# The second block's input projection as three fp32r products of split operands

## What is computed

```
xn = rmsnorm(h, g_mix)                      # 512 x 1024
z  = xn @ w_in + b_in                       # 1024 -> 1536
a, gate, p = z[:, :512], z[:, 512:1024], z[:, 1024:]
# conv group: GLU -> causal depthwise conv, 31 taps -> LayerNorm -> swish
u = a * sigmoid(gate); v = conv31(u) + b_dw; y_conv = silu(layernorm(v))
# pool group: 4 groups of 128 channels, trailing mean over 2, 4, 8, 16 tokens minus the token, then a 128x128 map
h = h + concat(y_conv, y_pool) @ w_out
h = h + swiglu(rmsnorm(h, g_ffn)); out = rmsnorm(h, g_final)
```

## Time and profile before

| what | value |
|---|---|
| median of 3 runs (lowest, highest) | 2475.74 us (2472.94, 2476.06) |
| the profiled execution: own time, span | 2474.01 us, 2472.2 us |
| granted PE clock, mean over the span | 0.892 of full |
| PE busy | 2221.1 us, 90% of the span |
| DVE busy | 627.3 us, 25% |
| ACT busy | 425.2 us, 17% |
| POOL busy | 32.7 us, 1% |

### The profile page before, as it was taken

How to read it: one execution, slowest core, us unless ns; L and a number is a source line. 1 busy time by engine, 2 the same in 40 slices (tenths; PEclk the granted TensorE clock), 3 DMA queues, 4 the chain that set the end, 5 groups by cost and what they waited for, 6 DMA issues and landing times.

```text
span 2472.2 us, 20613 instructions
## 1 busy us (share of the span) xinstructions
PE 2221.1 (90%) x8798; PEld 1295.5 (52%) x8798; DVE 627.3 (25%) x1011; ACT 425.2 (17%) x654; POOL 32.7 (1%) x42
## 2 busy tenths in 40 slices
PE   4977999899887898989989898989998998999997
PEld 2544454444574444444444444444343466888785
DVE  4251324232222111111111111011102943222233
ACT  2133534410010000000000000000011023222222
POOL 0000000000000000000000000000003000000000
PEclk9988999998787888888988888888989998999998
DMA  8210111034633897979979797989974113323210
GB/s 303 68 35 17 51 35 52 17 111 153 247 136 148 342 396 319 385 320 401 398 316 394 315 388 317 385 342 392 391 316 165 53 34 103 102 86 102 85 51 34
DMA packets 143792, 513.44 MB, mean 208 GB/s; under 512 B 7891, under 2 KB 70355, under 8 KB 107731
## 3 DMA queue, kind: packets, MB, share of 16 engines
q1 hardware_dynamic: 141632, 503.35, 52.8%
q10 hardware_dynamic: 2070, 8.78, 0.9%
HBM read 510.00 MB, written 2.10 MB: 207 GB/s over the span
## 4 chain that ended last, share of the span: by engine, by line
PE 88%; DVE 6%; ACT 3%; issue 2%; DMA 1%; POOL 0%; SPq 0%; ACTq 0%; DVEq 0%; POOLq 0%
PE ps L878 18%; PE ps L411 13%; PE ps L910 11%; PE ps L839 9%; PE ps L416 6%; PE ps L1053 5%; PE ps L1012 3%; PE ps L1014 3%; PE ps L1013 3%; PE ps L860 2%; PE ps L621 2%; DMA ring<-in_ada_w 1%; DVE work L1745 1%; PE ps L566 1%; PE ps L676 1%
## 5 line engine op out<-in xcount | busy, mean ns | idle before, releaser
L411 PE MATMUL ps<-work,ring 128*128 128x512 f32 x784 | 344.0, 597 | 0.8 <-DVE work L1589 0.8
L878 PE MATMUL ps<-work 128*64 128x512 f32 x1136 | 288.1, 595 | 0.0
L839 PE MATMUL ps<-work 128*128 128x64 f32 x1024 | 218.2, 416 | 62.8 <-DVE work L1712 62.8
L839 PEld LDWEIGHTS ps<-work 128*128 128x128 f32 x1024 | 215.2, 326 | 76.1 <-DVE work L1712 76.1
L411 PEld LDWEIGHTS ps<-work,ring 128*128 128x128 f32 x784 | 149.1, 192 | 187.3 <-issue 185.6
L878 PE MATMUL ps<-ring,work 128*64 128x512 f32 x912 | 238.1, 592 | 0.0
L878 PEld LDWEIGHTS ps<-work 128*64 128x64 f32 x1136 | 97.2, 138 | 158.3 <-issue 158.1
L1322 ACT ACTIVATE work<-ps 64x512 f32<-64x512 f32 x64 | 32.6, 585 | 749.1 <-PE ps L878 749.1
L878 PEld LDWEIGHTS ps<-ring,work 128*64 128x64 f32 x912 | 80.0, 137 | 126.7 <-issue 126.7
L416 PE MATMUL ps<-ring,work 128*128 128x256 f32 x640 | 142.0, 385 | 0.9 <-ACT work L1351 0.9
L1012 PE MATMUL ps<-xh,wh 128*128 128x512 f32 x352 | 138.0, 392 | 1.0 <-issue 1.0
(11 more groups left out here) (229 smaller groups left out, 2027.9 us busy)
## 6 DMA issues: line engine op xcount, KB each, us to landing
work<-in_w_exp_gate SPq DMA_DIRECT2D x71, 1024.0 KB, 12.7
work<-in_w_exp_up SPq DMA_DIRECT2D x71, 1024.0 KB, 10.8
ring<-in_w_exp_down SPq DMA_DIRECT2D x64, 1024.0 KB, 15.4
work<-in_w_exp_down SPq DMA_DIRECT2D x64, 1024.0 KB, 15.1
ring<-in_w_exp_up SPq DMA_DIRECT2D x57, 1024.0 KB, 9.6
ring<-in_w_exp_gate SPq DMA_DIRECT2D x57, 1024.0 KB, 11.7
ring<-in_w_in SPq DMA_DIRECT2D x27, 1024.0 KB, 7.6
ring<-in_ada_w SPq DMA_DIRECT2D x24, 1024.0 KB, 5.8
```

Source lines behind the costliest of these rows:

```text
L411: i = e.matmul(bank(bk), piece(key)[:, off + k, 128 * j:128 * j + 128], rhs(k), start=(k == 0), stop=(k == nk - 1))
L839: p = e.matmul(bank(5 - k // 4, 64, 64 * (k % 4)), at(XS2 + 1024 * c + 128 * k, 128), at(OH[z] + 64 * c, 64), start=(c == 0), stop=(c == 3))
L878: p = e.matmul(PS[64 * gu:64 * gu + 64, fb, :], at(XET[z] + 64 * k, 64), flat(key)[:, 512 * fb:512 * fb + 512], start=(k == 0), stop=(k == 7))
```

## The change

Each fp32 matmul of the projection becomes three fp32r matmuls: high part of the weights times high part of `xn`, high times low, and low times high (`dense_i2`, in place of `dense_T`). The parts are made so:

- `IH`, eight 128x512 blocks, on ACT, and `IL` (the rest `xn - IH`) on DVE, in the loop that copies `xn(k)` out of PSUM. `IL` takes the room of `xn` itself.
- the high part of each weight piece, `i2_hi(n)` on ACT, into one of two rooms of 128x2048 (`IWH`); the second of them is slot 5 of the ring.
- the low part, `i2_lo(n)`, in place in the piece's slot: pieces 0 and 1 on DVE, pieces 2 to 5 on GpSimd behind the 31 diagonal matrices.

A unit of PE waits for the low part of its piece, and u0 also waits block by block for `IL`. `i2_hi(n)` for n of 2 and more waits until PE is done with piece n - 2. The tail of the ring plan uses slots 0 to 4 for the first ten pieces, and SP waits for all twelve units before it loads `("ff", 0)` into slot 5. The places in ACT's program: `i2_hi(0)` ahead of the loop over k, `i2_hi(1)` behind it, 2, 3 and 4 ahead of the sigmoids of the second, third and fourth GLU pair, 5 behind the fourth.

```diff
--- before.py
+++ after.py
@@ -90,6 +90,9 @@
 YP = PSB + 2048 + 64
 PLT = [YP + 2048, YP + 2048 + 544]
 XS3, XS4 = U, XNT
+IXH = PLT[1] + 544
+IWH = [IXH + 4096, SLOT[5]]
+assert IWH[0] + W <= AR
 HIDO = WORK
 TQ = HIDO + FT * 512
 XHO = TQ + 2048
@@ -127,7 +130,7 @@
     cycle = (10, 11, 12, 5, 0, 3, 1, 2, 4, 6, 7, 8, 9)
     slots += [cycle[i % 13] for i in range(len(ex))]
     tail = [("i2", c) for c in (3, 1, 2, 0, 5, 4)] + [("o2", n) for n in range(4)] + [("ff", f) for f in range(33)]
-    slots += [i % 6 for i in range(len(tail))]
+    slots += [0, 1, 2, 3, 4, 0, 1, 2, 3, 4] + [(5, 0, 1, 2, 3, 4)[i % 6] for i in range(33)]
     keys += ex + tail
     uses, plan = {}, {}
     before = {}
@@ -180,7 +183,7 @@
     "mg_ga mg_gb mg_pa mg_pb mg_sa mg_sb mg_a mg_b mg_m ar_pe ar_a ad_d "
     "wo_pe wo_t wo_x rt_pe rt_e rt_d "
     "x_g x_oh x_xa x_xd x_ow x_ot x_oc x_gu x_sl x_hd x_ht x_hc x_dn x_ym x_cb x_ca "
-    "pads dg i2_pe gl_sg gl_u cv_pe cv_a cv_d pw_in pw_o po_pe po_y mu_pe dv sqv vr_pe ln_a y_d y_a "
+    "ix_h ix_l iw_h iw_d iw_p pads dg i2_pe gl_sg gl_u cv_pe cv_a cv_d pw_in pw_o po_pe po_y mu_pe dv sqv vr_pe ln_a y_d y_a "
     "o2_pe o2_x sx_h sx_l fs_h fs_l fs_p ff_pe ff_s ff_m hs_h hs_l dn_pe dn_e fin_x fin_a fin_o"
 ).split()
 
@@ -250,6 +253,9 @@
         XH, XL = part("xh", XHO, 4096), part("xl", XLO, 4096)
         WH = [part(f"wh{i}", WO + 4096 * i, 2048) for i in range(2)]
         WL = [part(f"wl{i}", WO + 4096 * i + 2048, 2048) for i in range(2)]
+        IH, IL = part("ih", IXH, 4096), part("il", XNT, 4096)
+        IWHI = [part(f"iwh{i}", o, 2048) for i, o in enumerate(IWH)]
+        IWLO = [part(f"iwl{i}", SLOT[i], 2048) for i in range(5)]
         hidf = part("hidf", HIDO, FT * 512, F32)
 
         csg, cact = small(8), small(8)
@@ -329,6 +335,7 @@
                 return piece(key, 2)
             return piece(key, 8)
 
+        I2C = (3, 1, 2, 0, 5, 4)
         I2 = {3: 3, 1: 4, 2: 7, 0: 8, 5: 10, 4: 12}
 
         def last_reader(key):
@@ -385,6 +392,9 @@
             for key, (slot, _, before) in plan.items():
                 if before is not None:
                     e.wait_ge(*last_reader(before))
+                if key == ("ff", 0):
+
+                    e.wait_ge(s["i2_pe"], 12)
                 if key == ("wo", 0):
                     e.wait_ge(s["mg_m"], 4)
                 if key[0] in ("eg", "eu") and before is None and slot >= 10:
@@ -921,24 +931,40 @@
             turn(XS3, [0, 1, 2, 3], lambda c: normed(3, c), t3_free, s["t_pe"])
 
             def xn_ready(k):
-                e.wait_ge(*turned_k(3, k))
+                e.wait_ge(s["ix_l"], k + 1)
+
+            def split_ready(c):
+                n = I2C.index(c)
+                e.wait_ge(*((s["iw_d"], n + 1) if n < 2 else (s["iw_p"], n - 1)))
+
+            def dense_i2(bk, c, j, each=None):
+                n = I2C.index(c)
+                hi, lo = IWHI[n % 2], IWLO[plan["i2", c][0]]
+                for k in range(KD):
+                    if each is not None:
+                        each(k)
+                    o, x = 256 * k + 128 * j, slice(512 * k, 512 * k + 512)
+                    e.matmul(bank(bk), hi[:, o:o + 128], IH[:, x], start=(k == 0), stop=False)
+                    e.matmul(bank(bk), hi[:, o:o + 128], IL[:, x], start=False, stop=False)
+                    p = e.matmul(bank(bk), lo[:, o:o + 128], IH[:, x], start=False, stop=(k == KD - 1))
+                return p
 
             def glu(m, i, cg, ca):
                 for u, c in ((2 * m, cg), (2 * m + 1, ca)):
                     if i in (3, 0):
-                        e.wait_ge(*got["i2", c])
+                        split_ready(c)
                     if u < 4:
 
                         e.wait_ge(*turned_k(3, 4 + u))
                     else:
                         e.wait_ge(s["gl_sg" if u % 2 == 0 else "gl_u"], (u - 4) // 2 + 1)
-                    dense_T(u % 4, ("i2", c), i % 2, xn, each=xn_ready if u == 0 else None).then_inc(s["i2_pe"], 1)
+                    dense_i2(u % 4, c, i % 2, xn_ready if u == 0 else None).then_inc(s["i2_pe"], 1)
 
             def pool_dense(u, g, c):
                 if g % 2:
-                    e.wait_ge(*got["i2", c])
+                    split_ready(c)
                 e.wait_ge(*{8: (s["gl_sg"], 3), 9: (s["gl_u"], 3), 10: (s["gl_sg"], 4), 13: (s["pw_in"], 2)}[u])
-                dense_T(u % 4, ("i2", c), g % 2, xn).then_inc(s["i2_pe"], 1)
+                dense_i2(u % 4, c, g % 2).then_inc(s["i2_pe"], 1)
 
             def pool_out(u, g):
                 e.wait_ge(s["pw_o"], 4 - g)
@@ -1333,12 +1359,34 @@
             gf = bass.AP(t["g_final_2"].tensor, t["g_final_2"].offset, [[0, 128], [1, 1024]])
             e.dma_start(at(GATE1, 1024), gf).then_inc(s["l_gf"], 16)
             rms(X, TP, st3, range(4), lambda c: None, s["r_a"])
-            turned(3, [0, 1, 2, 3], lambda k, src: e.activation(xn(k), src, ACT.Copy, scale=vcol("gmix", k)), lambda: None)
+
+            def i2_hi(n):
+                key = ("i2", I2C[n])
+                e.wait_ge(*got[key])
+                if n >= 2:
+                    e.wait_ge(s["i2_pe"], I2[I2C[n - 2]])
+                e.activation(IWHI[n % 2][:, :], flat(key), ACT.Copy).then_inc(s["iw_h"], 1)
+
+            i2_hi(0)
+            for k in range(KD):
+                if k % 2:
+                    e.wait_ge(*turns(3, k))
+                    e.activation(xn(k), bank(k % 4), ACT.Copy, scale=vcol("gmix", k)).then_inc(s["t_a"], 1)
+                e.wait_ge(*turned_k(3, k))
+                e.activation(IH[:, 512 * k:512 * k + 512], xn(k), ACT.Copy).then_inc(s["ix_h"], 1)
+            i2_hi(1)
 
             e.wait_ge(*turns(3, 7))
             for m, i in enumerate((3, 2, 0, 1)):
+                if m == 1:
+                    i2_hi(2)
+                elif m == 2:
+                    i2_hi(3)
+                elif m == 3:
+                    i2_hi(4)
                 e.wait_ge(s["i2_pe"], 2 * m + 1)
                 e.activation(at(TP + 512 * m, 512), bank(2 * m % 4), ACT.Sigmoid, bias=vcol("bin", 4 + i)).then_inc(s["gl_sg"], 1)
+            i2_hi(5)
             e.wait_ge(s["cv_pe"], 1)
             e.activation(at(CV + 1536, 512), bank(6), ACT.Identity, bias=vcol("bdw", 3)).then_inc(s["cv_a"], 1)
 
@@ -1759,7 +1807,22 @@
 
             e.wait_ge(s["x_ca"], 64)
             rms(3, X, XS3, st3, range(4), lambda c: None)
-            turned(3, [0, 1, 2, 3], lambda k, src: e.tensor_scalar(xn(k), src, vcol("gmix", k), None, ALU.mult))
+
+            def i2_lo(n):
+                c = I2C[n]
+                e.wait_ge(s["iw_h"], n + 1)
+                e.tensor_tensor(IWLO[plan["i2", c][0]][:, :], flat(("i2", c)), IWHI[n % 2][:, :].bitcast(F32), ALU.subtract).then_inc(s["iw_d"], 1)
+
+            for k in range(KD):
+                if k % 2 == 0:
+                    e.wait_ge(*turns(3, k))
+                    e.tensor_scalar(xn(k), bank(k % 4), vcol("gmix", k), None, ALU.mult).then_inc(s["t_d"], 1)
+                x = slice(512 * k, 512 * k + 512)
+                e.wait_ge(s["ix_h"], k + 1)
+                e.tensor_tensor(IL[:, x], xn(k), IH[:, x].bitcast(F32), ALU.subtract).then_inc(s["ix_l"], 1)
+                if k == 1:
+                    i2_lo(0)
+            i2_lo(1)
             e.wait_ge(*turns(3, 7))
             e.memset(raw(U, [(542, 4), (1, 30)]), 0.0).then_inc(s["pads"], 1)
             e.memset(raw(PSB, [(528, 4), (1, 16)]), 0.0).then_inc(s["pads"], 1)
@@ -1900,6 +1963,10 @@
             e.wait_ge(s["x_ca"], 64)
             for k in range(31):
                 e.tensor_scalar(at(DG + 128 * k, 128), ident, at(O_VEC + VEC["wdw"][0] + 93 + k, 1), None, ALU.mult).then_inc(s["dg"], 1)
+            for n in range(2, 6):
+                c = I2C[n]
+                e.wait_ge(s["iw_h"], n + 1)
+                e.tensor_tensor(IWLO[plan["i2", c][0]][:, :], flat(("i2", c)), IWHI[n % 2][:, :].bitcast(F32), ALU.subtract).then_inc(s["iw_p"], 1)
             e.wait_ge(s["fs_h"], 1)
             e.tensor_tensor(WL[0][:, :], flat(("ff", 0)), WH[0][:, :].bitcast(F32), ALU.subtract).then_inc(s["fs_p"], 1)
```

## The result

The changed kernel takes 2493.69 us (median of 4 runs, 2493.19 to 2494.59), the kernel before 2475.9 (2472.94 to 2476.24). The ratio is 1.0075 with a 95% interval of 1.0057 to 1.0092: 17.8 us slower. 2489.8 was forecast, with a range of 2481 to 2498.

The account below looks back on a forecast made before the run. DVE's taps were taken as the bound: start +3.4 us, GpSimd's holds 13.2 plus 0.3, 2.8 back behind the taps, +14.1 in sum; on the profiled 2474.01 that gives 2488.1, with 1.7 to the median 2489.8, range 2481 to 2498.

Parts of the forecast that it names:

- DVE bounds the stage, not PE: In the second block's mixer, DVE's 66.85 us of taps decide; PE cuts behind u3 are worth next to nothing.
- GpSimd holds the taps, 13.2 us plus 0.3: GpSimd's weight splits stall DVE's taps: three whole splits at 4.4 us each, plus 0.3 at the first.
- Rival 1: DVE's taps run untouched beside GpSimd: output projection 0.6 us later, 2476.3 us, no change; chance 12%.
- The start, +3.4: Up to u3's end: the new splits delay it to 1922.3 from 1918.9, with PE's own saving of 5.7 included.
- the twin: The feed-forward start, a similar loop whose profile rows were used to price the projection's start.
- PE's clock at u1: At the projection's second unit: half clock for some 4 us would add 2 us; only a bound, not summed.
- GpSimd's diagonal instructions: At the start, 31 instructions beside DVE's new subtractions: nothing added, upper bound 3 us.
- 2.8 us back behind the taps: From the last tap to the output projection: 24.85 us instead of 27.68, with PE at half clock for 4 us.
- From the output projection on, nothing changes.: The output projection and everything after it were costed at nothing, only shifted by the same amount.
- Rival 2: GpSimd gets in only where taps pause; splits 4 and 5 slip to their end: +21 us, 2497; chance 10%.
- Rival 3: PE, not DVE, ends last at the mean, so its cheaper units count: about -6.5 us, 2469; chance 6%.

Follow-up runs that it names:

- the narrow splits: The changed kernel with GpSimd's four weight splits cut to 8 of 2048 columns, low parts of pieces 2 to 5 left out; 2480.2 us, ratio 1.0021.
- the probes: The kernel before plus four 128x2048 GpSimd instructions on constants among DVE's taps (two subtractions, a multiplication, a memset); 2487.03 us, ratio 1.0047.
- the combined version: Against the changed kernel: weight splits moved earlier, none on GpSimd, u10 ahead of the mean, work behind the taps reordered, five spare matmuls; 2470.63 us, ratio 0.9979.
- the new order: u10 ahead of mean matmuls, subtractions right behind the mean, windows later, variance ahead of u13; 2489.71 us on the changed kernel, 2477.65 on the kernel before.
- the two combined versions: The combined version (2470.63 us), and the same with pool_window(2) moved into DVE's wait for Exp and three spare matmuls around the fourth mean matmul (2470.41 us).

## Why the prediction held, by its own steps

Profile against profile the forecast was +14.1 us and the measured difference +18.8. The 4.7 us between them are 2.3 at the start, 0.8 behind the taps, 1.7 in the output projection and 0.5 outside these stretches, less 0.5 in the taps.

**DVE bounds the stage, not PE.** Shown. With twelve units cheaper and no low part of the weights computed the time was that of the kernel before, with 66.87 us of taps, and what came back behind them went to half clock. The kernel is faster only where the start and the part behind the taps are changed as well.

**GpSimd holds the taps, 13.2 us plus 0.3.** Shown, by the narrow splits (-13.0 us in the stretch) and by the probes in a kernel without the change. A hold measures 4.1 to 4.3 us, 4.4 was forecast. Rival 1 is refuted by the same runs.

**The start, +3.4.** The mechanism was right, the sum 2.3 us short. Up to u1 the twin's rows fitted to 0.3 us (1905.31 in the trace, 1904.97 by my sum once the stage's start is 0.98 earlier). The term that was mis-sized is PE's clock at u1: priced at nothing with 2 us as its upper bound, it took 1.6 in five profiles and nothing in two. GpSimd's diagonal instructions cost the new subtractions at most 0.12 us each, as the earlier trace rows had it.

**2.8 us back behind the taps.** 1.98 came back. I gave PE half clock for 4 us there; the trace has 5.5, from 2003.5 to 2009, which is 0.75 us more.

**"From the output projection on, nothing changes."** This step failed. The projection took 57.19 us instead of 55.51. In the kernel before PE idled 1.58 us ahead of the last pool map and its clock stayed; with a shorter u13 it idled 2.86 us there, from 2024.25 to 2027.11, and its clock fell. Three spare matmuls brought 55.51 back.

**Rival 2, starvation** (10%). Its mechanism exists: a two-input GpSimd instruction that asked inside the alternating taps was kept out for 12 to 18 us in four runs. It did not arise in the changed kernel, since the third split asked at 1943.66, 0.06 us after the first of the 26 taps had started, and came in. And its price was wrong. I had it slip to the end of the taps; in fact the 14 single taps let it in 20 us earlier, and the time did not grow.

**Rival 3, PE's saving counts.** Refuted for this kernel. In the combined version it counts for the part behind the taps only: the new order there brings nothing without it.

What stays open: why u0's half clock lasts longer in some executions than in others, and whether the shorter gap that it leaves is what spares u1; why the one-input multiplication came in among the alternating taps; and the 1.4 us by which the feed-forward part took longer in the changed kernel's profile; between the other profiles it differs by up to 1.2 us, so nothing is read from it.

## What to carry to other kernels

Before giving work to an idle GpSimd, look at what DVE does beside it. Here both read SBUF, and DVE's instructions had two inputs there, so one waited for the other's whole instruction, and the idle engine's slower instruction was the longer hold: 4.2 us for work that DVE does in 2.3. Find the engine whose work ends last at the join, here the last tap, and ask first whether the change moves that point; of PE's 17 us of savings 2 came back behind the join in the old order, and 5 to 7 in the two combined versions. And an engine that is made faster idles. In the changed kernel's profile PE was at half clock behind each idle stretch of 1.86 us or more in this stage, and that cost 1.7 us at u1 and 1.7 at the output projection.

## What the runs showed of the hardware

- The hold works both ways, and who wins went with how closely DVE's instructions follow each other. With taps 0.79 us apart, GpSimd came in behind the tap under way; with taps 0.66 us apart, a two-input GpSimd instruction waited 12.3, 14.4, 14.4 and 17.6 us in four runs. At the very start of such a stretch (0.06 us in) or right behind another hold it did come in, and a one-input multiplication came in three taps into one.
- A GpSimd memset of 128x2048 (1.80 us) cost the taps beside it nothing; a one-operand multiplication 3.39 us, a subtraction 4.13.
- A gap of 1.86 to 2.32 us on PE ahead of u1 was followed by 3.4 us at half clock in five profiles, a gap of 1.59 or 1.62 us by none in two. Seven profiles don't show that the length decides.
